# First attention's output split into its two halves where it is made; projection row begun in the last head pair; norm vectors loaded as rows

## The reference

```
layer 0: h += neighbourhood_attention(rmsnorm(h, norm_mix[0])) @ a_w_o   # 16 heads of 64, window 8 x 16, bias table, meta keys
         h += swiglu(rmsnorm(h, norm_ffn[0]), w1, w3, w2)                # hidden 2816
layer 1: h += gqa_attention(rmsnorm(h, norm_mix[1])) @ b_w_o             # 16 query heads, 4 key heads, axial rotary
         h += swiglu(rmsnorm(h, norm_ffn[1]), w1, w3, w2)
out = rmsnorm(h, norm_final), grid tokens only
```

## Time and profile before

| | |
|---|---|
| median of three runs | 3090.8 us |
| profiled execution, its own time | 3092.26 us |
| its span | 3090.5 us |
| PE busy with matmuls | 2853.5 us, 92% |
| DVE, ACT, POOL busy | 42%, 21%, 43% |
| chain that ended last | PE 81%, DVE 9%, issue 3%, DMA 2% |

### The profile page before, as it was taken

The page is one execution under the profiler, slowest core; times in us unless marked ns, Lnnn a source line. Parts: engine busy times, 40 slices in busy tenths (PEclk is TensorE's granted clock), DMA queues, the critical chain, the costliest instruction groups (busy, mean ns, idle before and its releaser), DMA issues.

```text
span 3090.5 us, 40619 instructions
## 1 busy us (share of the span) xinstructions
PE 2853.5 (92%) x15386; PEld 2358.5 (76%) x15386; DVE 1289.7 (42%) x1621; ACT 655.7 (21%) x1126; POOL 1342.0 (43%) x1389
## 2 busy tenths in 40 slices
PE   4899999699999999999997599999699999999994
PEld 4788888499999999999886344444478888888883
DVE  2244444434223232225656566665352322223335
ACT  3243343411000000002100355554210000000001
POOL 1556555344444444444321266554254444444440
PEclk8899999899999999999999699999899999999996
DMA  6222121311111111112221100000311111111111
GB/s 171 49 61 60 51 54 44 132 48 45 44 44 45 47 49 48 45 48 93 63 68 49 56 1 35 36 1 14 145 44 43 53 48 48 46 44 46 50 44 59
DMA packets 233411, 167.68 MB, mean 54 GB/s; under 512 B 30880, under 2 KB 215840, under 8 KB 232624
## 3 DMA queue, kind: packets, MB, share of 16 engines
q1 hardware_dynamic: 212208, 123.03, 14.1%
q10 hardware_dynamic: 21056, 42.57, 3.9%
HBM read 136.69 MB, written 29.32 MB: 54 GB/s over the span
## 4 chain that ended last, share of the span: by engine, by line
PE 81%; DVE 9%; issue 3%; DMA 2%; ACT 1%; ACTq 1%; SPq 1%; POOL 0%; DVEq 0%; POOLq 0%
PE PS L602 58%; PE PS L715 8%; PE PS L921 3%; DVE nmx L1581 2%; PE PS L933 2%; PE PS L758 2%; PE PS L794 2%; PE PS L734 2%; DVE rcp L1624 2%; PE PS L879 1%; SPq L370 1%; DMA oraw<-o_spill 1%; PE PS L854 1%; PE PS L631 1%; DMA bias_rows<-vt 1%
## 5 line engine op out<-in xcount | busy, mean ns | idle before, releaser
L429 POOL TENSOR_TENSOR wh<-wraw,ones 128x512 fp32r<-128x512 f32 (+1 forms) x456 | 412.5, 905 | 1307.6 <-PE PS L602 1117.7
L602 PE MATMUL PS<-uh,wh 128*128 128x348 f32 (+1 forms) x2120 | 528.3, 349 | 23.6 <-POOL wl L432 10.2
L432 POOL TENSOR_TENSOR wl<-wraw,wh 128x512 fp32r<-128x512 f32 (+1 forms) x456 | 514.1, 1127 | 35.8
L602 PE MATMUL PS<-ul,wh 128*128 128x348 f32 (+1 forms) x2120 | 523.3, 346 | 0.0
L602 PE MATMUL PS<-uh,wl 128*128 128x348 f32 (+1 forms) x2120 | 522.5, 346 | 0.0
L602 PEld LDWEIGHTS PS<-uh,wh 128*128 128x128 f32 x2120 | 371.4, 189 | 61.2 <-issue 22.2
L602 PEld LDWEIGHTS PS<-ul,wh 128*128 128x128 f32 x2120 | 373.6, 189 | 31.9
L602 PEld LDWEIGHTS PS<-uh,wl 128*128 128x128 f32 x2120 | 371.7, 188 | 30.4
L1355 DVE TENSOR_TENSOR h<-PS,h 128x1044 f32<-128x1044 f32 (+1 forms) x192 | 236.9, 1234 | 334.3 <-PE PS L602 334.3
L1019 ACT ACTIVATE at<-at 128x1044 f32<-128x1044 f32 (+1 forms) x44 | 47.1, 1070 | 864.6 <-DVE at L1367 864.6
L602 PE MATMUL PS<-gh,wh 128*128 128x348 f32 (+1 forms) x880 | 223.3, 351 | 1.6 <-DVE h L1355 1.6
(11 more groups left out here) (187 smaller groups left out, 3766.2 us busy)
## 6 DMA issues: line engine op xcount, KB each, us to landing
wraw<-in_ffn_w SPq DMA_DIRECT2D x176, 256.0 KB, 2.9
wraw<-in_ffn_w SPq DMA_DIRECT2D x176, 128.0 KB, 2.2
wraw<-in_a_w_qkv SPq DMA_DIRECT2D x48, 256.0 KB, 2.8
biasb<-bias_rows SPq DMA_DIRECT2D x256, 36.0 KB, 1.9
oraw<-o_spill ACTq DMA_DIRECT2D x16, 522.0 KB, 6.6
h<-h_spill ACTq DMA_DIRECT2D x16, 522.0 KB, 10.5
qkv_spill<-tq ACTq DMA_DIRECT2D x12, 522.0 KB, 2.7
h_spill<-h SPq DMA_DIRECT2D x8, 522.0 KB, 6.8
```

The costliest lines, as they stand in the source:

```text
L429: nc.gpsimd.tensor_tensor(wh[:, slot, 0:w], wraw[:, slot, 0:w], ones[:, 0:1].to_broadcast([P, w]), ALU.mult).then_inc(s_whi, 1)
L432: nc.gpsimd.tensor_tensor(wl[:, slot, 0:w], wraw[:, slot, 0:w], wh[:, slot, 0:w].bitcast(F32), ALU.subtract).then_inc(s_wrd, 1)
L602: mm = nc.tensor.matmul(PS[:, set_ + c, 0:cw], w, x[k][:, c * cw:(c + 1) * cw], start=(first and i == 0 and ti == 0), stop=(last and i == ...
```

## The change

- The norm vectors are loaded as 40 rows of 128 into `graw`, transposed by PE into bank 0 and copied by DVE to `gains`. The fill of `bias_rows` is issued by ACT ahead of the x loop; its 16 table writes are issued by SP, behind the weights of q. SP's order becomes: table writes, weights of k, spill of `h`, `load_bias(0)`, weights of v and of the next q, `load_bias(1)`.
- x is transposed into banks 6, 7 and 4, 5 in turn, one signal per tile; DVE copies all eight chunks of a tile in one instruction, ACT only squares.
- `o_copy` writes the high half to `ohb`; a new `o_lo` on DVE makes the low half in `olb` from the same bank; both are spilled. `pv` waits for `o_lo`. For the last pair both go to chunk 7 of `uh` and `ul`.
- When the last q, k, v unit is done (in the last pair), SP reloads chunks 0 to 6 of `uh` and `ul` from the spills. PE runs seven of the eight chunks of the projection's first row as fillers in steps 5 to 8 of the last pair, the eighth after it, and the seven other rows as straight code (`proj_first`). `oraw`, `oh`, `ol` are left to layer 1.
- In layer 0 the FFN reads its input from new tiles `yh`, `yl`, and keeps its gated values in chunks 4 to 7 of `uh` and `ul`; ACT waits for the end of the FFN's units before it writes chunks 6 and 7 of the next `uh`.

```
+O_FILL = [14, 15, 16, 17, 19, 20, 22]
...
 HID = 2816
...
+                at1 = sb("at1", [P, 2, TP], F32, st)
...
+            with ExitStack() as st:
+                yh = sb("yh", [P, KC, TP], F32R, st)
+                yl = sb("yl", [P, KC, TP], F32R, st)
+                at0 = sb("at0", [P, 2, TP], F32, st)
+                sqf0 = sb("sqf0", [P, 2, TP], F32, st)
+            at, sq_ffn, sq_wo = [at0, at1], [sqf0, sqf1], [sqf0, oraw]
+            u_hi, u_lo = [uh, yh, uh, uh], [ul, yl, ul, ul]
+
+
+            gh = [[uh[:, 6:8, :], uh[:, 4:6, :]], [gh1[:, 0, :, :], gh1[:, 1, :, :]]]
+            gl = [[ul[:, 6:8, :], ul[:, 4:6, :]], [gl1[:, 0, :, :], gl1[:, 1, :, :]]]
         with ExitStack() as st:
...
+            ohb = sb("ohb", [P, TP], F32R, st)
+            olb = sb("olb", [P, TP], F32R, st)
             small = sb("small", [P, 4, 4], F32, st)
...
             fetch_chunk(0, w_qkv, 0)
+            sp.wait_ge(s_bfill, 16)
+            for c in range(CB):
+                sp.dma_start(bias_rows[:, c, 4:19, c + 1:c + 32], A["a_rel_bias"][0],
+                             allow_slow_non_contiguous=True).then_inc(s_brow, 16)
+            fetch_chunk(2, w_qkv, D)
             sp.wait_ge(s_pad, 3)
             sp.wait_ge(s_xra, 9)
-            sp.wait_ge(s_xrb, 9)
             for m in range(KC):
                 sp.dma_start(h_spill[:, m, :], h[:, m, :]).then_inc(s_hsp, 16)
-            fetch_chunk(2, w_qkv, D)
             load_bias(0)
-            load_bias(1)
             fetch_chunk(4, w_qkv, 2 * D)
             fetch_chunk(6, w_qkv, P)
+            load_bias(1)
             for p in range(NPAIR - 1):
                 fetch_chunk(6 * p + 8, w_qkv, D + P * (p + 1))
...
+            sp.wait_ge(s_un, U_WO[0])
+            for k in range(KC - 1):
+                sp.wait_ge(s_osp0, 32 * (k + 1))
+                sp.dma_start(uh[:, k, :].bitcast(F32), oh_spill[:, k, :]).then_inc(s_ox[k // 4], 16)
+                sp.dma_start(ul[:, k, :].bitcast(F32), ol_spill[:, k, :]).then_inc(s_ox[k // 4], 16)
...
                         for j in range(2):
-                            pe.wait_ge(s_or, KC * l + 4 * (j + 1))
+                            pe.wait_ge(s_or, 4 * (j + 1))
                             unit(n + j, j, set_, ohc, olc, range(4 * j, 4 * j + 4), j == 0, j == 1, l)
 
...
                 n = P if i < 8 else META
                 pe.wait_ge(s_xl[i], 16)
-                for f in range(2):
-                    if i:
-                        pe.wait_ge(s_xrb if f else s_xra, i)
-                    for c in range(4):
-                        k = 4 * f + c
-                        mm = nc.tensor.transpose(PS[:, 6 + f, c * n:(c + 1) * n],
-                                                 xt[0:n, i, k * P:(k + 1) * P], ident[0:n, 0:n])
-                    mm.then_inc(s_xt, 1)
+                if i >= 2:
+                    pe.wait_ge(s_xra, i - 1)
+                for k in range(KC):
+                    mm = nc.tensor.transpose(PS[:, X_BANK[i % 2] + k // 4, k % 4 * n:(k % 4 + 1) * n],
+                                             xt[0:n, i, k * P:(k + 1) * P], ident[0:n, 0:n])
+                mm.then_inc(s_xt, 1)
+            pe.wait_ge(s_const, 1)
+            pe.wait_ge(s_xra, 9)
             pe.wait_ge(s_pad, 3)
...
+            def o_filler(k):
+
+                if k in (0, 4):
+                    pe.wait_ge(s_ox[k // 4], 32 * (4 - k // 4))
+                if k == 7:
+                    pe.wait_ge(s_ol, 3 * NPAIR)
+                filler(U_WO[0], k, G_WO[0])
 
...
+                    pe.wait_ge(s_ol, 3 * p + j // 2)
                 if j == 4:
                     for hd in range(2):
...
+                            o_filler(O_FILL.index(k))
                     scores(p, v)
                     if p == 0 and v == 0:
...
+            o_filler(7)
+            proj_first()
             ffn(0)
 
...
+                    if k == 2 and m >= 6:
+                        act.wait_ge(s_un, U_FF[0] + 168 + KC)
+                    nc.scalar.activation(u_hi[k][:, m, 0:t], h[:, m, 0:t], ACT.Copy,
...
                         act.dma_start(h_spill[:, m, :], h[:, m, :]).then_inc(s_hsp, 16)
                 root(2 * l + 2)
 
             def proj_out(l):
-                act.wait_ge(s_osp, 16 * (KC + NG * l))
-                for m in range(OR):
-                    act.dma_start(oraw[:, m, :], o_spill[:, m, :]).then_inc(s_old[m], 16)
+                if l:
...
+                        act.dma_start(oraw[:, m, :], o_spill[:, m, :]).then_inc(s_old[m], 16)
...
-            act.dma_start(gains[:, 1, :], A["norm_ffn"][0].rearrange("(k p) -> p k", p=P),
-                          allow_slow_non_contiguous=True).then_inc(s_const, 16)
-            act.dma_start(gains[:, 2, :], A["norm_mix"][1].rearrange("(k p) -> p k", p=P),
...
+            act.wait_ge(s_zero, 1)
+            act.dma_start(bias_rows.rearrange("h c a e -> (h c a e)").rearrange("(p n) -> p n", p=P),
+                          vt[:, :, :].rearrange("p a b -> p (a b)")[:, 0:NH * CB * ARR * EW // P]
+                          ).then_inc(s_bfill, 16)
+            act.wait_ge(s_pad, 3)
             for i in range(9):
...
-                                     ACT.Copy).then_inc(s_xrb, 1)
-                if i == 0:
-                    act.wait_ge(s_pad, 3)
                 if i >= 2:
...
-                if i == 0:
-                    act.wait_ge(s_zero, 1)
-                    act.dma_start(bias_rows.rearrange("h c a e -> (h c a e)").rearrange("(p n) -> p n", p=P),
-                                  vt[:, :, :].rearrange("p a b -> p (a b)")[:, 0:NH * CB * ARR * EW // P]
-                                  ).then_inc(s_bfill, 16)
-                if i == 3:
-                    act.wait_ge(s_bfill, 16)
-                if 3 <= i <= 6:
-                    for c in range(4 * (i - 3), 4 * (i - 2)):
...
-                    act.wait_ge(s_osp, 16 * p)
+                    act.wait_ge(s_osp0, 32 * p)
                 n = 512 if i < 2 else META
-                nc.scalar.activation(ob[:, 512 * i:512 * i + n], PS[:, 5, 0:n], ACT.Copy).then_inc(s_ob, 1)
+                dst = ohb if p < NPAIR - 1 else uh[:, KC - 1, :]
+                nc.scalar.activation(dst[:, 512 * i:512 * i + n], PS[:, 5, 0:n], ACT.Copy).then_inc(s_ob, 1)
 
             def o_spilled(p):
                 act.wait_ge(s_ob, 3 * p + 3)
-                act.dma_start(o_spill[:, p, :], ob[:, :]).then_inc(s_osp, 16)
+                act.dma_start(oh_spill[:, p, :], ohb[:, :].bitcast(F32)).then_inc(s_osp0, 16)
+                act.wait_ge(s_ol, 3 * p + 3)
+                act.dma_start(ol_spill[:, p, :], olb[:, :].bitcast(F32)).then_inc(s_osp0, 16)
...
                 t_copy(NPAIR - 1, 8, hd)
             o_copy(NPAIR - 1, 2)
-            o_spilled(NPAIR - 1)
             proj_out(0)
...
+            dve.wait_ge(s_gt, 1)
+            nc.vector.tensor_copy(gains[:, :, :].rearrange("p g k -> p (g k)"), PS[:, 0, 0:5 * KC]).then_inc(s_const, 1)
...
-                dve.wait_ge(s_xt, 2 * i + 1)
-                nc.vector.tensor_copy(h[:, 0:4, P * i:P * i + n],
-                                      PS[:, 6, 0:4 * n].rearrange("p (c n) -> p c n", n=n)).then_inc(s_xra, 1)
+                dve.wait_ge(s_xt, i + 1)
+                nc.vector.tensor_copy(h[:, :, P * i:P * i + n].rearrange("p (b c) n -> p b c n", b=2),
+                                      PS[:, X_BANK[i % 2]:X_BANK[i % 2] + 2, 0:4 * n]
+                                      .rearrange("p b (c n) -> p b c n", n=n)).then_inc(s_xra, 1)
...
+            def o_lo(p, i):
+                dve.wait_ge(s_ob, 3 * p + i + 1)
+                if i == 0 and p:
+                    dve.wait_ge(s_osp0, 32 * p)
+                n = 512 if i < 2 else META
+                a = slice(512 * i, 512 * i + n)
+                hi, lo = (ohb, olb) if p < NPAIR - 1 else (uh[:, KC - 1, :], ul[:, KC - 1, :])
+                nc.vector.tensor_tensor(lo[:, a], PS[:, 5, 0:n], hi[:, a].bitcast(F32),
+                                        ALU.subtract).then_inc(s_ol, 1)
...
+                    if v == 0 and p:
+                        o_lo(p - 1, 1)
                     for hd in range(2):
                         bias(p, v, hd)
                     for hd in range(2):
                         norm(p, v, hd)
+                    if v == 0 and p:
+                        o_lo(p - 1, 2)
+                    if v == 6:
+                        o_lo(p, 0)
...
+            o_lo(NPAIR - 1, 1)
+            o_lo(NPAIR - 1, 2)
```

More of the change, by code:

```diff
@@ L475, in _ @@
             split_unit(5)
-            nc.gpsimd.memset(ob[:, :], 0.0).then_inc(s_zero, 1)
+            for t in (ohb[:, :].bitcast(F32), olb[:, :].bitcast(F32)):
+                nc.gpsimd.memset(t, 0.0).then_inc(s_zero, 1)
             def strips(p):
@@ L612, in dense, with chunks @@
                     unit(n + j, j, set_, xh, xl, range(4 * j, 4 * j + 4), j == 0, j == 1, l)
```

(47 more changed lines are left out.)

82 lines of the change are left out of this document (40 added, 42 removed).

## The result

The changed kernel takes 3048.5 us (median of 4 runs, 3048.0 to 3050.0), the kernel before 3094.6 beside it (3088.6 to 3098.8): a ratio of 0.986, 95% interval 0.984 to 0.988. The profiled execution took 3048.0 with a span of 3046.2; that of before had 3090.5. So 44.3 us of span went, where 64.9 were forecast. Four marks divide the span; the "forecast" column is the prediction's working.

What follows compares the result with a forecast made beforehand. PE was taken to bound middle pairs and projection, leaving its idle time at the start and after attention: 40.3 + 24.6 = 64.9 us off 3092.3 gives 3027.4, predicted 3027, range 3014 to 3048.

Steps and rivals of the forecast that it cites:

- `h` complete at 22.5: Start, x into `h`: PE's transposes set the pace, `h` complete at 22.5 instead of 52.7, gain 30.2 us.
- From `h` to the end of the first scores, 36.6 us: Start: first product 2.75 us behind `h`, then 33.9 us to the end of pair 0's first scores at 59.1.
- rival (a): Start: x keeps 3.89 us a tile, `h` complete and its spill issued at 39 instead of 22.5; 3044 us, chance 0.14.
- The v row right behind the scores: Start, pair 0: v's weights ready before PE wants them, so the v row follows the scores; gain 10.2 us.
- Rival (b): Start: SP's queue is the bound and v's weights come 10 us late, at 69; 3037 us, chance 0.10.
- Middle pairs, 1.5 us lost: Seven middle pairs: `o_lo` delays the next bias on DVE, 0.25 us in each of 6 pairs, 1.5 lost (0 to 5).
- Last pair, 8.7 us longer: Last pair: fillers of 10.0 us with 2.0 in PE's idle time, 8.0 net, plus 0.7 for DVE's part.
- Wait for `h`, 1.2 us: Projection's start: DVE adds row 0 till 600.0, row 2 needs its banks at 598.8; 1.2 us lost (0 to 9).
- Projection without a gap, the middle and the first FFN at nothing: After the last pair: PE without a gap over 1.5 us to 668; first FFN's new tiles and ACT's wait cost nothing.
- Rival (c): Last pair and projection: `h` or the reloads late, second pair of rows or fillers stall 9 to 12 us; 3038, chance 0.08.
- (d): Whole span: the granted clock falls with PE's breaks gone, 28 us per cent, 3100 at 2.6 per cent; chance 0.03.
- (e): Projection: its rows still wait for something counted as done, a part of pair 7; 3050 us, chance 0.03.

Runs made afterwards that it cites:

- e3: Changed kernel with the 16 table writes on ACT's queue behind its first `uh`, and v's weights ahead of pair 0's bias: 3047.7 us, ratio 0.986.
- e6: Changed kernel with one filler in each last-pair step from the third on, and a semaphore for each reloaded part: 3042.8 us, ratio 0.983.
- e7: Kernel before the change, with only the norm vectors loaded as rows, transposed by PE and copied by DVE: 3075.3 us, ratio 0.995.
- e1: Changed kernel with each x tile loaded from 128 consecutive rows, so its output differs: 3034.7 us, ratio 0.981.
- e11: Changed kernel with the edits of e10 and of e3 together: 3029.3 us, ratio 0.980.
- e10: Changed kernel with x read with its 16 columns as slowest dimension, plus the edits of e4 and e6: 3032.4 us, ratio 0.981.
- e5: Changed kernel with the seven fillers taken out of the last pair and the projection's whole first row run behind it: 3044.7 us, ratio 0.985.
- e4: Changed kernel with a semaphore for each reloaded chunk of `h`, so DVE's first add waits for chunk 0 only: 3045.4 us, ratio 0.985.

## Why the prediction was wrong

The direction held, and of the mechanism the order of the stages; three waits were mis-sized or missing: 3027 forecast, range 3014 to 3048, measured 3048.5. (The range's lower end was worked out as 3018 and put at 3014 without a term for it.) Of 20.6 us too few, 14.3 are in the start, 0.2 in the middle pairs, 5.6 in pair 7 and the projection, and 0.5 behind it.

- **`h` complete at 22.5: failed, 11.3 us.** I let TensorE set the pace, with 1.28 us a tile for x, from a reload of the spilled `h`. x, read in 8 pieces, came at 2.97, and at 3.22 to 4.26 in four other executions of the same load. The two ends stood in the prediction, 22.5 and 39.5; I took the cheap end because the elements beside x were gone. That reason isn't borne out: without any elements e3 and e6 came at 4.26 and 4.15, slower than the 3.89 beside them, and a packet of x took 0.231 and 0.235 us there and 0.226 in the kernel before. e7's x, at about 3 us a tile, lies within this spread. e1 shows that the pace is in the read: with consecutive rows `h` is complete at 21.1. The rule on turns that the prediction cites from the Trainium skill (DMA: Bandwidth & Descriptors, Queues, rings and completion order) is not decided by these runs, since x is as slow with nothing to take turns with. The step that failed is carrying a rate from one transfer to another of the same size without looking at its pieces.
- **From `h` to the end of the first scores, 36.6 us: failed, 6.4 us.** It took 43.0. I had the spill behind the table writes and k's weights in SP's sum, but only to find when v's weights come; that DVE's read of q waits for the landing (13 us behind the last issue) was missing. The wait is 5.80, of which 4.4 are its own, and the k row behind it ran partly at the lower clock (14.48 us, 2.8 more than before). The scores were 0.7 shorter. The sum on SP failed as well: it had the table writes end at 22 and cost 10 us, but SP's issues of the meta tokens, of q's weights and of the first table write took over 5 us each, the writes went from 21.73 to 37.5, and the spill was issued at 38.83, 5.0 behind `h`. That is the 39 set down as rival (a)'s sign, here for another reason. That DVE waits for the landing is in the chain of waits, and e11, in which it doesn't, begins its fills 2.7 us earlier than e10, from which it differs in e3's edit alone.
- **The v row right behind the scores: held.** The row took 11.65 us and not 14.12, as the clock was back by then: 2.4 us better than the sum, with the 1 us charged for `load_bias(1)` not seen either. 11.3 + 6.4 - 2.4 - 1.0 is the 14.3. Rival (b), SP's queue as the bound, had its mechanism half right: the queue delayed the spill, and v's weights were not waited for.
- **Middle pairs, 1.5 us lost: held.** From the fills to the read of v of pair 7 it is 421.9 us, before 420.1: 1.7.
- **Last pair, 8.7 us longer: 10.2.** The fillers, given 8.0 net, cost 7.5 (e5). The other 2.7 us stand also without fillers; 0.7 of them are the low halves. What I had at nothing can be read in part: DVE's first two normalisings are 0.9 us longer, and the first full product runs at a lower clock (2.67 us in e5, 1.96 before). The first is not the reload's doing, since the middle pairs have it too: `o_lo` pushes both normalisings right behind the start of POOL's two operations on `bm`. No run takes `o_lo`, the reload or POOL's work away, so how the 2.0 divide is not shown.
- **Wait for `h`, 1.2 us: failed, 4.1 us with what hangs on it.** The load landed 15.1 us after its first issue (562.76 to 577.88), where 13.0 was forecast. The first add also waited for all eight chunks, where I had the adds run on from the end of row 0 and the stall at row 2. PE stood for 2.86 us ahead of its next row and then ran 70.51 us for 432 matmuls, 1.8 more than at e4's pace (504 in 80.18), at a clock of 0.98. e4 gets all of it back.
- **Projection without a gap, the middle and the first FFN at nothing: held**, but for the wait for `h`. Rival (a) (x keeps 3.89 us a tile, 3044) was nearer to what x did than the forecast, but 3044 comes without the other misses, so that it lies close to the result is in part luck. Rival (c) (`h` or the reloads late, 9 to 12 us) came for `h`, at 4.1; (d) and (e) are ruled out: 580 to 649 is busy throughout, and the mean clock is 0.970 (before 0.966).

## What to carry to other kernels

Take a load's rate only from a row with the same pieces on both sides; where there is none, the forecast is a range, and the first thing to try is a read that is one block of memory. Read it from more than one execution: here the same load took 2.97 to 4.26 us a tile. Follow each store that must land before a buffer is overwritten to the reader that it holds, and see what stands ahead of it in its queue. Work that is put into a pair's gaps pays best when it is spread over all of its steps, and a reload should release its reader by the chunk.

## What the hardware showed unexpectedly

- Loads of 512 KB in 128 rows of 4 KB moved at 412 GB/s in one block, at 134 to 190 in 8 pieces on half of the engines, and at 240 to 254 in 16 pieces on all of them (SP's queue, 12 to 17 us). A DMA share near 1.0 does not mean a full rate: a packet took from 0.142 to 0.320 us.
- The same load in 8 pieces, in five executions, took 0.165, 0.183, 0.222, 0.231 and 0.235 us a packet, always at half of the engines' time. Nothing in the kernels differs up to there; the cause is open.
- Loading 16 partitions at a time was as slow as the slowest of these: x moved at 144 GB/s in that window (0.72 MB in 5 us), with 0.320 us a packet.
- DVE's operation on 416 columns in SBUF took 1.15 and 1.06 us beside POOL's operations on `bm` at a DMA share of 1.03, and 1.16 and 1.07 beside them at 0.38. With no operation of POOL beside it (227.99 us) it took 0.44. So the length goes with POOL and not with the DMA traffic.
